# Moving scans, page loads and weight conversions within a hybrid decoder step

## What is computed

```python
def attn_prompt(...):                   # for each block of 128 queries
    score = einsum(relu(iq . ik), iw);  causal mask
    idx = top_k(score, 256)             # the kernel finds the 256th score bit by bit
    p = softmax(q . k[idx] / 8 + t5_bias)
    return p @ v[idx]
def attn_sample(...):                   # 8 rows; keys and values from 64 pages of 128 tokens
    ...the same over cache_k[page_table], cache_v[page_table] and the new row
def gla_chunk(S0, q, g, k, v):          # chunks of 64 rows
    b = cumsum(g);  o = (masked q.k exp(b_t - b_s)) @ v + (q exp(b)) @ S0
    S_new = exp(b[-1]) * S0 + (k exp(b[-1] - b)).T @ v
def out_merge(...):
    mix = concat([a_out * silu(a_gate), rms_norm(h_out) * silu(h_gate)])
    return x + mix @ w_out
```

## Time and profile before

| | |
|---|---|
| median of 3 runs | 775.99 us (774.6 to 779.53) |
| the profiled execution | 779.53 us, span 777.8 us |
| mean granted TensorE clock | 0.996 |
| PE busy | 745.2 us (96% of the span) |
| DVE, ACT, POOL busy | 552.1, 414.8, 384.8 us (71%, 53%, 49%) |
| DMA | 83.56 MB, mean 107 GB/s |

### The profile page before, as it was taken

The page is one execution under the profiler, slowest core; times in us unless marked ns, Lnnn a source line. Parts: engine busy times, 40 slices in busy tenths (PEclk is TensorE's granted clock), DMA queues, the critical chain, the costliest instruction groups (busy, mean ns, idle before and its releaser), DMA issues.

```text
span 777.8 us, 20014 instructions
## 1 busy us (share of the span) xinstructions
PE 745.2 (96%) x7480; PEld 689.0 (89%) x7480; DVE 552.1 (71%) x1112; ACT 414.8 (53%) x1260; POOL 384.8 (49%) x572
## 2 busy tenths in 40 slices
PE   3999999999999999999999999999999999999998
PEld 3889789799999999999998999978788878898998
DVE  5837778888888999998997946788646477554121
ACT  5755874445375787667564746654445564321110
POOL 3555336348644494649676345259860526410220
PEclk9999999999999999999999999999999999999999
DMA  7430211310102312131203446497483543432632
GB/s 232 151 86 18 75 43 61 103 40 17 56 2 83 97 42 83 59 109 42 96 2 89 143 125 177 112 281 200 111 267 113 164 152 118 157 109 66 232 99 85
DMA packets 69926, 83.56 MB, mean 107 GB/s; under 512 B 20458, under 2 KB 55962, under 8 KB 69578
## 3 DMA queue, kind: packets, MB, share of 16 engines
q1 hardware_dynamic: 65146, 68.68, 28.3%
q0 software_dynamic: 4688, 13.64, 6.1%
HBM read 64.95 MB, written 17.34 MB: 106 GB/s over the span
## 4 chain that ended last, share of the span: by engine, by line
PE 60%; DVE 20%; issue 13%; ACT 4%; DMA 1%; POOL 1%; DVEq 1%; SPq 0%; ACTq 0%
PE psum L2345 14%; PE psum L1360 11%; PE psum L2342 9%; PE psum L1293 4%; DVE flag_count L2075 4%; PE psum L1309 4%; PE psum L2259 3%; DVE bit_kept L2088 2%; DVE flag L2075 2%; PE psum L1267 2%; PE psum L1273 2%; PE psum L1271 2%; PE psum L2195 1%; DVE flag_count L975 1%; PE psum L1330 1%
## 5 line engine op out<-in xcount | busy, mean ns | idle before, releaser
L2345 PE MATMUL psum<-w_high,xT_high 128*128 128x256 f32 x640 | 183.1, 286 | 1.0 <-ACT psum L1841 0.5
L2345 PE MATMUL psum<-w_low,xT_high 128*128 128x256 f32 x640 | 179.5, 280 | 0.0
L2345 PE MATMUL psum<-w_high,xT_low 128*128 128x256 f32 x640 | 179.3, 280 | 0.0
L557 POOL TENSOR_TENSOR w_low<-w_raw,w_high 128x256 fp32r<-128x256 f32 (+1 forms) x144 | 105.5, 770 | 65.0 <-ACT w_high L1714 56.7
L2345 PEld LDWEIGHTS psum<-w_high,xT_high 128*128 128x128 f32 x640 | 120.4, 188 | 3.8 <-ACT psum L1841 0.9
L2345 PEld LDWEIGHTS psum<-w_high,xT_low 128*128 128x128 f32 x640 | 120.4, 188 | 0.4
L2345 PEld LDWEIGHTS psum<-w_low,xT_high 128*128 128x128 f32 x640 | 120.5, 188 | 0.0
L2075 DVE TENSOR_SCALAR_CACHE_REDUCE flag_count<-scores,candidate 128x512 f16<-128x512 f32 (+2 forms) x96 | 96.8, 1008 | 0.0
L2342 PE MATMUL psum<-xT_high,w_high 128*128 128x392 f32 (+5 forms) x280 | 93.5, 334 | 0.0
L2342 PE MATMUL psum<-xT_low,w_high 128*128 128x392 f32 (+5 forms) x280 | 90.6, 324 | 0.0
L2075 DVE TENSOR_SCALAR_CACHE_REDUCE flag<-scores,candidate 128x384 f16<-128x384 f32 (+2 forms) x96 | 84.1, 876 | 9.3 <-DVE candidate L2091 8.7
(11 more groups left out here) (337 smaller groups left out, 1857.9 us busy)
## 6 DMA issues: line engine op xcount, KB each, us to landing
w_raw<-in_w_main SPq DMA_DIRECT2D x40, 512.0 KB, 4.0
x_rows<-in_x_prompt SPq DMA_DIRECT2D x8, 512.0 KB, 5.7
page_keys<-in_cache_kt SPq DMA_DIRECT2D x32, 128.0 KB, 4.1
page_keys<-in_cache_kt POOLq DMA_DIRECT2D x32, 128.0 KB, 3.8
page_values<-in_cache_v SPq DMA_DIRECT2D x32, 128.0 KB, 4.2
page_values<-in_cache_v POOLq DMA_DIRECT2D x32, 128.0 KB, 3.7
x_res<-in_x_prompt SPq DMA_DIRECT2D x32, 128.0 KB
out<-y_rows SPq DMA_DIRECT2D x32, 128.0 KB
```

The lines of the kernel that those rows point to most:

```text
L557: last = gp.tensor_tensor(WL[:, u % 2, 4 * h + k, 0:w], raw(u)[:, h, k, 0:w], f(WH[:, u % 2, 4 * h + k, 0:w]), ALU.subtract)
L2345: last = pe.matmul(ps(BANK[n], w, rows(i)), x[:, k, row0(i):row0(i) + rows(i)], ww[:, sl, k, 0:w], start=first, stop=final)
```

## The change

It changes seven tables and three places in the code. Two rounds of DVE's search move from ahead of scan(1) to behind it; keep(4) and try(5) stand behind 15 rounds instead of 14, keep(5) and try(6) behind 17 instead of 18; the flag matmul of try 4 follows job 52 instead of 50. POOL issues key groups 7, 9 and 11 inside or right behind the state update, 13 and 15 behind it, and value groups 5 and 7 ahead of all gain and gate steps. The last two value steps go from m = 34 to 35 (`SOFT_AT` is 19), mix(2) from 40 to 39, mix_rows(0) and (1) from 30 and 32 to 33; the two halves of an output weight unit are converted together at m = 37 and 45 instead of at 36, 38 and 44, 46. The waits of `high_half` move into `high_w`.

```diff
--- before.py
+++ after.py
@@ -71,14 +71,14 @@
 HGRN_AT = KEYS_AT[-1] + 1
 MASK_AT = [HGRN_AT + 1 + c for c in range(3)]
 SOFT_AT = MASK_AT[-1]
-VALUES_AT = [SOFT_AT + x for x in (6, 8, 10, 10, 12, 14, 15, 15)]
+VALUES_AT = [SOFT_AT + x for x in (6, 8, 10, 10, 12, 14, 16, 16)]
 
 
 ORDER = [7, 6, 5, 4, 3, NT, 2, 1, 0]
-MIX_AT = [35, 37, 40, 42, 45, 48, 53, 59]
-MIX_ROWS_AT = [30, 32, 38, 41, 44, 47, 52, 57]
+MIX_AT = [35, 37, 39, 42, 45, 48, 53, 59]
+MIX_ROWS_AT = [33, 33, 38, 41, 44, 47, 52, 57]
 OUT_AT = [41, 43, 45, 47, 49, 52, 54, 55, 58, 62]
-HIGH_AT = {36: (0, 0), 38: (0, 1), 44: (1, 0), 46: (1, 1)}
+HIGH_AT = {37: 0, 45: 1}
 
 
 def width(u):
@@ -134,9 +134,9 @@
 ITEMS_AT = {n: [4 * g + x for g in gs for x in range(4)] for n, gs in GROUPS.items()}
 KEYS_ROWS_AT, SAMPLE_AT, SAMPLE_SUM_AT = 5, 21, 23
 
-FLAGS_AT = {33: 0, 39: 1, 43: 2, 47: 3, 50: 4, 57: 5, 68: 6, 73: 7}
-KEEP_AT = [6, 8, 10, 12, 14, 18, 23, 26]
-SCAN_AT = [5, 16]
+FLAGS_AT = {33: 0, 39: 1, 43: 2, 47: 3, 52: 4, 57: 5, 68: 6, 73: 7}
+KEEP_AT = [6, 8, 10, 12, 15, 17, 23, 26]
+SCAN_AT = [5, 14]
 
 
 def lows_for(t, h):
@@ -785,13 +785,14 @@
                     gp.tensor_tensor(S0T[:, b, :, :], S0T[:, b, :, :], spread(FS, b), ALU.mult)
                     last = gp.tensor_tensor(VBT[:, b, :, :], VBT[:, b, :, :], spread(KSS, b), ALU.mult)
                     if b == 3:
-                        load_key_pages(gp, numbers, 11)
+                        load_key_pages(gp, numbers, 7)
                 link(last)
                 for b in range(SB):
                     last = gp.tensor_tensor(S0T[:, b, :, :], S0T[:, b, :, :], VBT[:, b, :, :], ALU.add)
                     if b == 3:
-                        load_key_pages(gp, numbers, 13)
+                        load_key_pages(gp, numbers, 9)
                 last.then_inc(s["sample_state_ready"], 1)
+                load_key_pages(gp, numbers, 11)
                 gp.wait_ge(s["sample_state_ready"], 1)
                 link(gp.memset(QHP[:, :, :], 0.0))
                 w = SB * NG * BR
@@ -829,10 +830,9 @@
             for hh in range(2):
                 gp.dma_start(VBT[hh * HD:(hh + 1) * HD, :, :, :].rearrange("p b j v -> p (b j v)"),
                              bass.AP(d_hv, hh * SB * NG * HD, [[0, HD], [1, SB * NG * HD]])).then_inc(s["states_in"], 16)
-            for n in (7, 9):
+            sample_state()
+            for n in (13, 15):
                 load_key_pages(gp, numbers, n)
-            sample_state()
-            load_key_pages(gp, numbers, 15)
             for hh in range(2):
                 gp.dma_start(s_sample[0].rearrange("b (j a) k v -> a k (b j) v", a=2)[hh],
                              S0T[hh * HD:(hh + 1) * HD, :, :, :].rearrange("p b j v -> p (b j) v"))\
@@ -844,13 +844,11 @@
             link(gp.tensor_scalar(MN[0:BR, 0:1], MN[0:BR, 0:1], 1.0 / HD, EPS, ALU.mult, ALU.add))
             inverse_root(gp, link, MN[0:BR, 1:2], MN[0:BR, 0:1], MN[0:BR, 2:3])
             gp.tensor_scalar(HOSM[0:BR, :], HOSM[0:BR, :], MN[0:BR, 1:2], 0.0, ALU.mult, ALU.add).then_inc(s["sample_hgrn_normed"], 1)
-            load_value_pages(gp, numbers, 3)
+            for n in (3, 5, 7):
+                load_value_pages(gp, numbers, n)
             for x in range(NT + 1):
                 gain(x)
                 gated(x)
-                if x == 1:
-                    for n in (5, 7):
-                        load_value_pages(gp, numbers, n)
                 if x == 2:
                     split_w(gp, NU)
                 if x == 5:
@@ -901,7 +899,7 @@
                 dst = XMIX[:, 4 * h:4 * h + 4, :] if i == NT else XH[:, 4 * h:4 * h + 4, row0(i):row0(i) + rows(i)]
                 act.activation(dst, src, ACT.Copy).then_inc(s["mix_high_ready"], 1)
 
-        def act_tail(act, link, high_w, high_half):
+        def act_tail(act, link, high_w):
             def sample(kind, b):
                 if kind == "hgrn":
                     act.wait_ge(s["sample_hgrn_ready"], 1)
@@ -918,7 +916,7 @@
                     act.activation(PSM[0:BR, 0:PAST + 1], PSM[0:BR, 0:PAST + 1], ACT.Exp, scale=HD ** -0.5,
                                    bias=SMS[0:BR, 1:2], accum_out=SMS[0:BR, 2:3]).then_inc(s["sample_exp_ready"], 1)
                 elif kind == "weights":
-                    high_half(NU + b[0], b[1])
+                    high_w(NU + b)
                 elif kind == "mix":
                     mix_high(act, b)
 
@@ -1697,16 +1695,6 @@
             def high_half(u, h):
 
                 w = width(u)
-                if h == 0 and u == 2:
-                    act.wait_ge(s["job_done"], IX_JOBS)
-                elif h == 0 and NU > u > 2:
-                    act.wait_ge(s["job_done"], JOB0[u - 1])
-                elif h == 0 and NU <= u < NU + 2:
-                    act.wait_ge(s["sample_values_done"], SB)
-                    if u > NU:
-                        act.wait_ge(s["sample_attn_out"], 16 * KVH)
-                elif h == 0 and u > NU + 1:
-                    act.wait_ge(s["out_done"], OEND[u - NU - 2])
                 if u == 1:
                     act.wait_ge(s[f"second_weights_in{h}"], 16)
                 else:
@@ -1715,6 +1703,18 @@
                     .then_inc(s["weights_high_ready"], 1)
 
             def high_w(u):
+
+                if u == 2:
+                    act.wait_ge(s["job_done"], IX_JOBS)
+                elif NU > u > 2:
+                    act.wait_ge(s["job_done"], JOB0[u - 1])
+                elif u == NU:
+                    act.wait_ge(s["sample_values_done"], SB)
+                elif u == NU + 1:
+                    act.wait_ge(s["sample_values_done"], SB)
+                    act.wait_ge(s["sample_attn_out"], 16 * KVH)
+                elif u > NU + 1:
+                    act.wait_ge(s["out_done"], OEND[u - NU - 2])
                 for h in range(2):
                     high_half(u, h)
 
@@ -1941,7 +1941,7 @@
                             act.activation(RS[:, 0, 0:1], IDN[:, 0:1], ACT.Exp)
                     if n == QUERIES_AT:
                         act_sample_queries(act)
-            act_tail(act, link, high_w, high_half)
+            act_tail(act, link, high_w)
 
 
         @block.vector
```

## The result

The changed kernel takes 790.45 us (median of 5 runs, 786.69 to 792.25), the kernel before 775.99 us. The ratio of all runs is 1.0168 (95% interval 1.014 to 1.0196): 1.7% slower, some 13 us, where the forecast had 8.

The account below looks back on a forecast made before the run. The prediction took TensorE (PE) as the bound, busy 745.2 of 777.8 us. Terms A 4.7, K 1.5 and M 1.8 summed to +8.0, hence 784.0 us on the median of 776.0; range 778.5 to 790.

Parts of the forecast that it names:

- The sign and the larger mechanisms: Whole kernel: slower by 8.0 us, through DVE's wait before the scan, late key pages and new waits at the mix.
- A: Search: DVE idles some 10 us before the second scan, PE stalls 3.2 us at job 57's flag, 1.5 clock loss: 4.7 us.
- K: Key pages: POOL issues group 7 behind eight state multiplications, so PE waits near 540: 1.5 us, bounds 0 to 1.9.
- M: Values, mix rows and output weights, heads 33 to 41: new waits less the old 2.46 us wait: +1.8, bounds -4.0 to +5.1.
- The case's own range: The forecast's own case, A to M as worked out with bounds: 781 to 787.5 us, chance 0.50.
- The remark that the later groups cost nothing: Key groups behind group 7 are used five and more heads later, slip about one place each, and were priced at nothing.
- The credit for the half clock: In M: 0.8 us credited for half the clock loss of 1.5 us behind the old wait near 640.
- Rival B: DVE's short pass L2088 behind round 17 starves behind POOL's stream; PE waits 5.1 us for try(7): 788 to 793, chance 0.17.
- The remark that the 9.40 us span two dozen POOL instructions: Said that DVE's 9.40 us L2088 in the kernel before spanned two dozen POOL instructions, against the skill's one-instruction lock.
- D: The wait near 640 and its half clock go (-4.0), with A nil by an earlier L1728 and K 0: 772 to 776, chance 0.08.

Follow-up runs that it names:

- scan_back: The changed kernel with the second scan behind 16 search rounds again (SCAN_AT = [5, 16]): 783.6 us, ratio 1.0102 to the kernel before.
- flag5_later: The kernel before with the change's search tables alone, and flag 5 behind job 59 instead of 57: median 780.57 us, ratio 1.0068 to the kernel before.
- mask_scan_later: The kernel before with the change's key group order alone, and DVE's sample mask scan at m=6 instead of 5: 780.44 us, ratio 1.0041.
- group7_first: The changed kernel with key group 7 alone back ahead of the state arithmetic: 787.16 us, ratio 1.0144 to the kernel before.
- tail_only: The changed kernel with search tables and key group order of the kernel before: 777.52 us, ratio 1.0023 to the kernel before.
- scan_15_pauses: The kernel before with the change's search tables, second scan behind 15 rounds, and memset pauses in POOL's stream: 775.15 us, ratio 0.9983.

## Why the prediction was right or wrong

**The sign and the larger mechanisms** were right. The time lies at the upper end of the stated range, 778.5 to 790, around 784.0: by the ratio it is 775.99 x 1.0168 = 789.0, while the median of 790.45 alone is just outside. Term by term, from the traces: A 4.7 forecast, the search part +5.4; K 1.5 forecast, the key part +5.8; M +1.8 forecast, the tail +1.1. So nearly all that was missing is K. That the search part came out so near to A is in part luck: PE won back 1.6 us up to 396, and lost 1.6 and 0.5 us again at two of DVE's later products, and the forecast had none of the three. The case's own range, 781 to 787.5, does not follow from the bounds given with A, K and M, which add up to 775.2 to 787.9.

**Term A** (4.7 us) was right in mechanism and size: DVE's 9.31 us before the scan, PE's 3.55 us at the flag matmul, and 1.2 us of half clock behind it. scan_back shows the scan's place as the cause and flag5_later the flag as the link to PE.

**The step that failed in the search part** was one that the prediction took for granted when it ended the working at job 57: that DVE's delay costs nothing afterwards. DVE was 4.8 us late at its own part of w_low (420.21 against 415.38), for which PE waited 0.18 us before and 1.80 now. That made 1.6 us. The matmul was among PE's waits in the kernel before, so it had nothing to spare, and I had not followed DVE's order up to its last product.

**Term K** failed most: 1.5 us forecast, 4.5 us of wait and 1.2 of half clock measured (bounds 0 to 1.9, with no half clock in them). The last issue of group 7 was placed by durations taken over from the kernel before, L785 at 0.61 us and v_spread's 12.6 us. The first failed by 2.0 us, since DVE's scan met POOL's arithmetic where before it had met issues (mask_scan_later shows it: 1.7 us of wait less). v_spread took 1.2 us longer in the changed kernel. Why was not tried: from its issue to the arithmetic it is 12.1 to 15.7 us in the traces here, and taking page loads away from beside it did not bring it below 12.6 (13.0, 13.8, 14.4 and 14.5 in the four kernels that issue none there), so nothing supports K's lower bound. The remark that the later groups cost nothing was true only because group 7's wait stood ahead of them (group7_first).

**Term M** (+1.8) was met, +1.8 for tail_only, but with an interval of +0.1 to +3.5 this says little. In the changed kernel the three new waits are 1.06, 1.12 and 1.37 us (forecast 1.6, 1.5 and 1.4), and the old one of 2.46 is gone, as forecast. Of the first, 0.7 us goes with the values back at m=34. The credit for the half clock is one that the kernel before collects or not by execution: runs of it have mean granted clocks from 0.993 to 1.0.

**Rival B** had 0.17. In the changed kernel's profiled execution the very pass that it named, behind the six of round 17, stood in the middle of POOL's stream and went through:

```profile
283.29 0.50 DVE L2088 SCALAR_TENSOR_TENSOR bit_kept<-count,bit_value 128x6 int32<-128x6 f32 x1
```

The longest pass near it took 1.84 us (at 292.37), and the flag of try(7) waited for nothing. The stream had come 1.0 us earlier (278.85 against 279.84), not 2. In flag5_later one execution shows B, and the times put it in four of ten. The mechanism was right. The price was of the right order: 5.1 us forecast with PE already 4.7 late, so 9.8 without, and 7.6 us there with a clock of 0.50 from 328 to 338 around it. Whether the changed kernel has it in some runs cannot be told from its times. The remark that the 9.40 us span two dozen POOL instructions is a misreading: of the stream's 24 they span the last 14. **D** would have needed an earlier L1728, which ended at the time forecast.

## What to carry to other kernels

When an engine that is not the bound gets a wait of several microseconds, follow its order on to every later product that the bound engine takes from it, and write down the slack of each; here the first cost 3.6 us and a later one 1.6. When a step moves to another place beside other engines, its old duration no longer holds: look what will run beside it there. And where the times fall into two groups, look in a trace of each for a mechanism before calling it noise; here only the upper group was profiled.

## What the runs showed of the hardware

- **A short DVE pass with two SBUF operands can be held up over many POOL instructions.** In the 14 traces 262 passes L2088 ran beside a two-operand POOL product. 35 of them took 1.8 to 9.40 us, all others under 0.82. Three of the 35 (1.84 us each) ended between two POOL products. The other 32, the longest of 8.05, 8.39, 9.38 and 9.40 us among them, ended within 0.03 us of the end of a POOL product behind which POOL paused for 0.18 us or more. The Trainium skill, SBUF — State Buffer, "Who interferes with whom", has an exclusive lock for one instruction, whichever starts first, and only against a GpSimd instruction that reads SBUF; in these traces the hold spans up to 14 POOL instructions. Which pass is caught differs from trace to trace, and no run shows what decides it. With POOL memsets (an operation that reads nothing) behind every two to four products none of 41 passes in two traces took over 0.76 us; the kernel before has two long ones and each of the other eleven traces three.
- **The reverse holds too:** DVE's scan over 8 x 1025, which reads two SBUF operands, kept one POOL product from ending for 2.0 us (2.60 instead of 0.61), in ten of the traces here. This agrees with the lock that the Trainium skill, SBUF — State Buffer, "Who interferes with whom", states. In the kernel before the scan ran beside four of POOL's DMA issues, which took their usual 2.90 us.
- **A half-clock stretch is not decided by the length of the wait alone.** It came with waits of 2.46, 3.55, 4.48 and 4.95 us; but in scan_15_pauses PE waited 2.49 us at 637.97 and the clock stayed full. In tail_only 0.82 was granted around three waits of 1.1 to 1.6 us, where the changed kernel, with three of 1.1 to 1.4, has 1.00 (641:656 above):

```profile
641.00:650.00 9.00, 9.00 (x81) 8.61 (x81) 7.70 (x15) 2.96 (x9) 4.99 (x5) 1.00 0.52 175
```

```profile
641.00:650.00 9.00, 9.00 (x69) 8.54 (x69) 7.24 (x16) 3.52 (x9) 6.40 (x8) 0.82 0.63 204
```

The first is scan_15_pauses, the second tail_only. With PE busy for all of the 9 us, 0.82 instead of 1.00 is some 1.6 us lost (an estimate: 0.18 of 9). That much of a difference between two executions can be this alone.
